# Odd mixer of a four-layer decoder on one Trainium2 core: the two softmax maps combined in one operation, the head norm taken per group inside the attention loop, its weight applied where the rows are transposed

## The reference, cut to what matters

```python
def diff_attention(q, k, v, lam):              # q, k: (B, S, H=8, 2, 64); v: (B, S, 8, 128)
    def block(qi):                             # 128 queries at a time
        s = jnp.einsum('bqhcd,bkhcd->bhcqk', qi, k).astype(jnp.float32) * scale
        p = jax.nn.softmax(s, axis=-1)
        a = p[:, :, 0] - lam * p[:, :, 1]
        return jnp.einsum('bhqk,bkhe->bqhe', a.astype(v.dtype), v)
    ...
def rms_norm(x, g):
    y = xf * lax.rsqrt(jnp.mean(jnp.square(xf), axis=-1, keepdims=True) + LN_EPS)
    return y.astype(x.dtype) * g

def odd_mixer(x, w_in, lam_p, subln_g, w_out, lam_init):
    q, k, v = jnp.split(x @ w_in, 3, axis=-1)
    q, k = rope(q), rope(k)                    # shortened
    lam = jnp.exp(jnp.sum(lp[0] * lp[1])) - jnp.exp(jnp.sum(lp[2] * lp[3])) + lam_init
    o = diff_attention(q, k, v, lam)
    o = rms_norm(o, subln_g) * (1.0 - lam_init)
    return o.reshape(B_, S, C_WIDTH) @ w_out
```

## Time and profile before

| what | value |
|---|---|
| executions timed | 3221.38, 3225.34, 3228.93 us; median 3225.34 us |
| the profiled execution's own time | 3220.99 us |
| its span in the trace, first to last instruction | 3219.2 us |
| mean granted clock of TensorE | 0.971 of full speed |
| PE busy | 3025.5 us (94%) |
| PEld, weight loads | 2511.7 us (78%) |
| POOL busy | 1751.4 us (54%) |
| DVE busy | 921.4 us (29%) |
| ACT busy | 645.0 us (20%) |
| the page's chain of work that ended last, PE's and DVE's share | 79% and 14% |

### The profile page before, as it was taken

The page is one execution under the profiler, slowest core; times in us unless marked ns, Lnnn a source line. Parts: engine busy times, 40 slices in busy tenths (PEclk is TensorE's granted clock), DMA queues, the critical chain, the costliest instruction groups (busy, mean ns, idle before and its releaser), DMA issues.

```text
span 3219.2 us, 35940 instructions
## 1 busy us (share of the span) xinstructions
PE 3025.5 (94%) x15048; PEld 2511.7 (78%) x15048; DVE 921.4 (29%) x1470; ACT 645.0 (20%) x1330; POOL 1751.4 (54%) x1472
## 2 busy tenths in 40 slices
PE   7889999999999897999999999899999998999998
PEld 6776778888887666788888887878888886788887
DVE  3535402311023295023100221833110056530102
ACT  1224212211010162122100121452010032420100
POOL 5540383566665503836666656423666665556664
PEclk9999999999999998999999999989999999899999
DMA  4221241322223202412322232002323222033232
GB/s 143 71 74 40 70 143 50 105 92 98 99 87 104 66 1 66 144 53 92 105 92 94 90 112 92 1 1 81 103 92 104 93 98 79 14 100 97 92 105 79
DMA packets 182498, 267.15 MB, mean 83 GB/s; under 512 B 6592, under 2 KB 145984, under 8 KB 182336
## 3 DMA queue, kind: packets, MB, share of 16 engines
q1 hardware_dynamic: 174240, 243.28, 22.9%
q10 hardware_dynamic: 8096, 21.56, 2.0%
HBM read 262.73 MB, written 2.10 MB: 82 GB/s over the span
## 4 chain that ended last, share of the span: by engine, by line
PE 79%; DVE 14%; POOL 3%; issue 1%; ACT 1%; DMA 1%; ACTq 0%; DVEq 0%; POOLq 0%
PE PS L464 23%; PE PS L465 23%; PE PS L466 23%; PE PS L785 3%; POOL wlo L2084 2%; DVE PS L665 2%; DVE x_row L660 1%; PE PS L771 1%; DVE nmx L1434 1%; PE PS L1324 1%; DVE xT_lo L566 1%; DVE x_row L672 1%; PE PS L917 1%; POOL whi L2079 1%; PE PS L549 1%
## 5 line engine op out<-in xcount | busy, mean ns | idle before, releaser
L2079 POOL TENSOR_SCALAR whi<-raw 128x1024 fp32r<-128x1024 f32 x460 | 485.7, 1076 | 1336.2 <-DMA raw<-ffn_w 270.0
L2084 POOL TENSOR_TENSOR wlo<-raw,whi 128x512 fp32r<-128x512 f32 x920 | 1188.5, 1328 | 0.0
L464 PE MATMUL PS<-xT_hi,whi 128*128 128x512 f32 (+1 forms) x2304 | 856.0, 372 | 41.4 <-DVE xT_lo L566 29.1
L465 PE MATMUL PS<-xT_lo,whi 128*128 128x512 f32 (+1 forms) x2304 | 848.7, 368 | 0.0
L466 PE MATMUL PS<-xT_hi,wlo 128*128 128x512 f32 (+1 forms) x2304 | 848.5, 368 | 0.0
L464 PEld LDWEIGHTS PS<-xT_hi,whi 128*128 128x128 f32 x2304 | 441.6, 192 | 118.1 <-DVE xT_lo L566 32.4
L465 PEld LDWEIGHTS PS<-xT_lo,whi 128*128 128x128 f32 x2304 | 441.6, 192 | 71.5 <-issue 2.4
L466 PEld LDWEIGHTS PS<-xT_hi,wlo 128*128 128x128 f32 x2304 | 441.4, 192 | 70.1
L464 PE MATMUL PS<-whi,xT_hi 128*128 128x512 f32 x672 | 264.5, 394 | 23.6 <-ACT a_pre L1025 16.3
L960 DVE TENSOR_TENSOR htmp<-sil,PS 128x512 f32<-128x512 f32 x88 | 56.5, 683 | 804.0 <-ACT sil L945 804.0
L464 PE MATMUL PS<-whi,h_hi 128*128 128x512 f32 x704 | 274.1, 389 | 0.0
(11 more groups left out here) (360 smaller groups left out, 3218.5 us busy)
## 6 DMA issues: line engine op xcount, KB each, us to landing
raw<-ffn_w SPq DMA_DIRECT2D x66, 1024.0 KB, 5.0
raw<-ffn_w_gu SPq DMA_DIRECT2D x44, 1024.0 KB, 5.1
raw<-ffn_w_down SPq DMA_DIRECT2D x22, 1024.0 KB, 5.0
raw<-mem_wkv SPq DMA_DIRECT2D x16, 1024.0 KB, 5.4
raw<-even_w_in SPq DMA_DIRECT2D x14, 1024.0 KB, 5.2
raw<-ev_w_in SPq DMA_DIRECT2D x14, 1024.0 KB, 5.3
raw<-odd_w_in SPq DMA_DIRECT2D x12, 1024.0 KB, 5.1
raw<-od_w_in SPq DMA_DIRECT2D x10, 1024.0 KB, 5.0
```

The source lines that it names most:

```text
L464: pe.matmul(o, lhs[0], rhs[0], start=start, stop=False, skip_group_check=True)
L465: pe.matmul(o, lhs[0], rhs[1], start=False, stop=False, skip_group_check=True)
L2079: pool.tensor_scalar(whi[b][:, cs], raw[b][:, cs], 1.0, 1.0, ALU.mult, ALU.mult).then_inc(panel_hi, 1)
L2084: m = pool.tensor_tensor(wlo[b][:, cs], raw[b][:, cs], whi[b][:, cs].bitcast(F32), ALU.subtract)
```

## The change

It does these things in `stage_odd`, and nothing in the other stages:

1. `combine` works without the first map's reciprocal. With sums s0 and s1 it forms the ratio -lam*s0/s1 (two instructions on one column) and then, in one instruction over 512 columns, map 1 times the ratio plus map 0. The result is s0 times the one before. The norm per head takes the factor out again, if its small constant is multiplied by s0 squared.
2. The norm moves into the loop, one group at a time. ACT squares the group's PSUM bank into `d_sq` (new instruction, 128x512, after the copy of unit 4g+5); `store` sums the squares per head on DVE, forms the constant times s0 squared, adds the two, waits for POOL, which raises the four columns to the power -0.5, and multiplies the bank by the result on its way to `d_row`. `store` comes two steps later (`behind` is 6 instead of 4), so groups 6 and 7 both come after the last unit.
3. The weight `subln_g` becomes one column (after the transpose a head's feature lies on the partition) and is applied, with 1 - LAM_INIT, in the copies behind the transposes: ACT's copy has it as scale, DVE's subtraction becomes one with a multiplication before it.
4. The passes after the loop (1392, 1395, 1448, 1452, 1455, 1456) are gone. With them goes the load of ACT's table for the root, which is now done in the layer norm of the output projection.
5. POOL gets the loop over the eight groups between the splits of the third and the fourth panel of the output weights.

```diff
-            pool_at.append(len(panels) + 2)
+            pool_at.append(len(panels) + (3 if st[0] == "odd" else 2))
...
+                m = act.activation(dst_hi[:, k0 + b:k0 + b + 4, 128 * t:128 * t + 128],
+                                   PS[:, bank + b // 4, :].rearrange("p (k c) -> p k c", k=4), ACT.Copy, scale=gain)
...
+                    m = dve.scalar_tensor_tensor(out=lo, in0=src, scalar=gain, in1=hi.bitcast(F32),
+                                                 op0=ALU.mult, op1=ALU.subtract)
...
-        def act_units(act, A, exps):
+        def act_units(act, A, exps, more=lambda u: None):
...
                     act.activation(A.pt(u)[:, 0:w], PS[:, A.ptb(u), 0:w], ACT.Copy).then_inc(pt_sb, 1)
+                    more(u)
...
-            behind = A.lag + 1
+            behind = A.behind
...
+            A.behind = 6
...
-                act_units(act, A, exps)
+                def squares(u):
+                    g = (u - 2) // 4
+                    if u < 5 or u % 4 != 1:
+                        return
+                    act.wait_ge(pv_done, A.u0 + 4 * g + 4)
+                    if g >= 2:
+                        act.wait_ge(sq_in, g - 1)
+                    act.activation(d_sq[:, g % 2, :], PS[:, A.ob(4 * g), :], ACT.Square).then_inc(sq_done, 1)
+                act_units(act, A, exps, squares)
+                squares(A.n + 1)
                 phase_end(act, "act")
                 load_next(act)
                 for t in range(NT):
-                    if t >= 3:
-                        act.wait_ge(sq_in, t - 2)
-                    act.activation(d_p[:, t % 3, :, :].rearrange("p a b -> p (a b)"), d_row[:, t, :], ACT.Square)\
-                        .then_inc(sq_done, 1)
-                act.wait_ge(sq_in, NT)
-                act.activation(rec[:, 0:32], rec[:, 32:64], ACT.Sqrt, scale=1.0 / 128, bias=eps_col[:, 0:1]).then_inc(sd_done, 1)
-                act_rows(act, 0, KD)
+                    act_turn(act, xT_hi, 0, KD, 2 * t, t, gain)
...
                 def combine(u):
                     dve.wait_ge(exp_done, A.u0 + u + 1)
-                    r0, r1, lr1 = (scol[:, o:o + 1] for o in range(24 + 4 * (u % 2), 27 + 4 * (u % 2)))
-                    step(dve.reciprocal(scol[:, 24 + 4 * (u % 2):26 + 4 * (u % 2)], rsum[:, 2 * u:2 * u + 2]))
-                    step(dve.tensor_tensor(lr1, r1, scol[:, 21:22], ALU.mult))
+                    ratio = scol[:, 24 + u % 2:25 + u % 2]
+                    step(dve.reciprocal(ratio, rsum[:, 2 * u + 1:2 * u + 2]))
+                    step(dve.scalar_tensor_tensor(out=ratio, in0=ratio, scalar=scol[:, 21:22],
+                                                  in1=rsum[:, 2 * u:2 * u + 1], op0=ALU.mult, op1=ALU.mult))
                     if u >= 3:
                         dve.wait_ge(pt_psum, A.u0 + u - 2)
-                    p1 = d_p[:, u % 3, 1, :]
-                    step(dve.tensor_scalar(p1, p1, lr1, None, ALU.mult))
-                    dve.scalar_tensor_tensor(out=d_a[:, u % 3, :], in0=d_p[:, u % 3, 0, :], scalar=r0,
-                                             in1=p1, op0=ALU.mult, op1=ALU.subtract).then_inc(p_ready, 1)
+                    dve.scalar_tensor_tensor(out=d_a[:, u % 3, :], in0=d_p[:, u % 3, 1, :], scalar=ratio,
+                                             in1=d_p[:, u % 3, 0, :], op0=ALU.mult, op1=ALU.add).then_inc(p_ready, 1)
...
                 def store(g, bank):
-                    return dve.tensor_copy(d_row[:, g // 2, 512 * (g % 2):512 * (g % 2) + 512], PS[:, bank, :])
+                    s0, ms, rstd_ = rsum[:, 8 * g:8 * g + 8:2], *rms_cols(g)
+                    heads = lambda ap: ap.rearrange("p (h d) -> p h d", h=4)
+                    dve.wait_ge(sq_done, g + 1)
+                    dve.tensor_reduce(ms, heads(d_sq[:, g % 2, :]), AX_X, ALU.add).then_inc(sq_in, 1)
+                    step(dve.scalar_tensor_tensor(out=rstd_, in0=s0, scalar=EPS, in1=s0, op0=ALU.mult, op1=ALU.mult))
+                    dve.wait_ge(sq_in, g + 1)
+                    dve.scalar_tensor_tensor(out=ms, in0=ms, scalar=1.0 / 128, in1=rstd_, op0=ALU.mult, op1=ALU.add)\
+                        .then_inc(rms_in, 1)
+                    dve.wait_ge(rms_root, g + 1)
+                    return dve.tensor_tensor(heads(d_row[:, g // 2, 512 * (g % 2):512 * (g % 2) + 512]), heads(PS[:, bank, :]),
+                                             rstd_.unsqueeze(2).to_broadcast([P, 4, 128]), ALU.mult)
...
+            def pool(pool):
+                for g in range(8):
+                    pool.wait_ge(rms_in, g + 1)
+                    ms, rstd_ = rms_cols(g)
+                    pool.tensor_tensor(rstd_, ms, rec[:, 16:20], ALU.pow).then_inc(rms_root, 1)
...
-                for t in range(NT):
-                    pe.wait_ge(rms_done, t + 1)
-                    pe_turn(pe, d_row[:, t, :], KD, 2 * t)
+                pe_rows(pe, d_row, 0, KD)
```

More of the change, by code:

```diff
@@ L201, in build @@
         d_pt = w("d_pt", [P, 2, 512])
-        d_sq = w("d_sq", [P, 512])
+        d_sq = w("d_sq", [P, 2, 512])
         w = Area("W")
@@ L551, in pe_turn, with act_turn @@
             m.then_inc(turned, 1)
-        def act_turn(act, dst_hi, k0, blocks, bank, t):
+        def act_turn(act, dst_hi, k0, blocks, bank, t, gain=1.0):
             n_turn["act"] += 1
@@ L557, in act_turn, with dve_turn @@
                 m = act.activation(dst_hi[:, k0 + b:k0 + b + 4, 128 * t:128 * t + 128],
-                                   PS[:, bank + b // 4, :].rearrange("p (k c) -> p k c", k=4), ACT.Copy)
+                                   PS[:, bank + b // 4, :].rearrange("p (k c) -> p k c", k=4), ACT.Copy, scale=gain)
             m.then_inc(hi_ready, 1)
-        def dve_turn(dve, dst_hi, dst_lo, k0, blocks, bank, t):
+        def dve_turn(dve, dst_hi, dst_lo, k0, blocks, bank, t, gain=None):
             n_turn["dve"] += 1
@@ L565, in dve_turn @@
             for b in range(0, blocks, 4):
-                m = dve.tensor_tensor(dst_lo[:, k0 + b:k0 + b + 4, 128 * t:128 * t + 128],
-                                      PS[:, bank + b // 4, :].rearrange("p (k c) -> p k c", k=4),
-                                      dst_hi[:, k0 + b:k0 + b + 4, 128 * t:128 * t + 128].bitcast(F32), ALU.subtract)
+                lo, hi = (dst[:, k0 + b:k0 + b + 4, 128 * t:128 * t + 128] for dst in (dst_lo, dst_hi))
+                src = PS[:, bank + b // 4, :].rearrange("p (k c) -> p k c", k=4)
+                if gain is None:
+                    m = dve.tensor_tensor(lo, src, hi.bitcast(F32), ALU.subtract)
+                else:
+                    m = dve.scalar_tensor_tensor(out=lo, in0=src, scalar=gain, in1=hi.bitcast(F32),
+                                                 op0=ALU.mult, op1=ALU.subtract)
             m.then_inc(lo_ready, 1)
@@ L733, in build @@
             lag = 3
+            behind = 4
             together = 1
@@ L1337, in stage_odd @@
                       lambda u: d_a[:, u % 3, :], lambda u: d_pt[:, u % 2, :], lambda u: u % 4 == 3)
+            A.behind = 6
             chunk = lambda c: slice(128 * c, 128 * c + 128)
             xs_ready, swapped, rope_done = S_("rope_in"), S_("rope_swapped"), S_("rope_done")
-            rms_done = S_("rms_done")
-            lam_in, lam_exp, sq_in, sq_done, sd_done = (S_(n) for n in (
-                "lam_sums", "lam_exp", "rms_sums", "rms_squares", "rms_root"))
+            lam_in, lam_exp, sq_in, sq_done, rms_in, rms_root = (S_(n) for n in (
+                "lam_sums", "lam_exp", "rms_sums", "rms_squares", "rms_in", "rms_root"))
+            gain = scol[:, 22:23]
+            rms_cols = lambda g: [rec[:, o:o + 4] for o in (8 * (g % 2), 8 * (g % 2) + 4)]
             def xs_in(n):
@@ L1403, in dve @@
                 dve.wait_ge(lam_exp, 1)
-                step(dve.tensor_tensor(scol[:, 20:21], scol[:, 18:19], scol[:, 19:20], ALU.subtract))
-                step(dve.tensor_scalar(scol[:, 21:22], scol[:, 20:21], LAM_INIT, None, ALU.add))
+                step(dve.tensor_tensor(scol[:, 20:21], scol[:, 19:20], scol[:, 18:19], ALU.subtract))
+                step(dve.tensor_scalar(scol[:, 21:22], scol[:, 20:21], -LAM_INIT, None, ALU.add))
+                step(dve.tensor_scalar(gain, pcol("subln_g"), 1.0 - LAM_INIT, None, ALU.mult))
+                dve.memset(rec[:, 16:20], -0.5)
                 dve.wait_ge(*loads["rope"])
@@ L1446, in dve @@
                 for t in range(NT):
[L1447 to L1452, removed]
-                for t in range(NT):
[L1454 to L1461, removed]
+                    dve_turn(dve, xT_hi, xT_lo, 0, KD, 2 * t, t, gain)
+            def pool(pool):
[3 more added lines that the diff above has]
+                    pool.tensor_tensor(rstd_, ms, rec[:, 16:20], ALU.pow).then_inc(rms_root, 1)
             def pe(pe):
@@ L1502, in pe @@
                 phase_end(pe, "pe")
-                for t in range(NT):
-                    pe.wait_ge(rms_done, t + 1)
```

(6 more changed lines are left out.)

2 lines of the change are left out of this document (1 added, 1 removed).

## The result

| | kernel before | changed kernel |
|---|---|---|
| median of four runs, us | 3224.67 | 3207.21 (3204.02 to 3210.88) |
| ratio, 95% interval | | 0.9945 (0.9928 to 0.9963) |
| profiled execution / span, us | 3220.99 / 3219.2 | 3204.02 / 3202.2 |
| first to last maximum of the odd mixer ("loop") | 89.70 | 89.21 |
| last maximum to first product of the output projection ("end") | 32.05 | 18.73 |

The forecast sum of 17.1 us met the profiled pair (17.0), and the forecast time of 3206 us the median. Only 13.8 us of the 17.0 lie in the changed stage, all but 0.5 of them at its end.

What follows compares the result with a forecast made beforehand. DVE was taken to bound the loop, PE 0.16 us behind per unit, with most to win in the norm's passes after it. 1.0 + 2.4 + 15.2 - 1.5 = 17.1 us gave 3203.9 or 3208.2; predicted 3206, range 3197 to 3220.

Steps and rivals of the forecast that it cites:

- first five units: Start of the odd mixer's loop: scalings go, but PE at its lower clock takes over as bound; 1.0 us gained.
- units 5 to 31: Rest of the odd mixer's loop, 26 units and 6 stores: 73.8 us before, 71.4 after, 2.4 gained.
- end, clock deduction taken off: Last maximum to output projection: 32.05 us falls to 16.83, 15.2 gained, less 1.5 for PE's clock falling before the transposes.
- outside the stage: Everything but the odd mixer: what lies behind it is only shifted as a whole; forecast 0.
- per group DVE now needs 4 x 2.18 + 2.46 = 11.18: Odd mixer's loop: four units and a store on DVE, still the bound against PE's 10.16; 11.40 before.
- P: In each store: hand-over to POOL, power and way back, hidden by nothing; 0.94 us, between 0.26 and 1.45.
- The three-operand product on one column: In each unit's combination on DVE: costed as the product it replaces, 0.20 us.
- Rival 1: Stores: POOL's power is slow and DVE waits eight times; at 5 us the kernel takes some 3240; 7%.
- Rival 2: End: PE reaches the transposes at its lower clock, costing 4.6 us instead of 1.5, 3209; 18%.
- Rival 3: First store: POOL must first fetch the power's routine, stalling DVE and PE once; 4 to 6 us, about 3211; 8%.
- Rival 4: Loop gives nothing or loses a little at P = 1.45; sum 13 us, 3210; within the forecast's own 62%.
- The table load: Layer norm of the output projection: the root's 1.28 us load moves there and costs nothing; first transposes 40.92 after projection start.

Runs made afterwards that it cites:

- e2_mult: Changed kernel with GpSimd multiplying where it takes the power, same 128x4 operands, so the norm is not computed; 3202.71 us, ratio 0.9932 to the kernel before.
- e5_after_again: The changed kernel run once more without an edit; 3210.32 us, ratio 0.9951 to the kernel before.
- e1_par128: Changed kernel with `subln_g` padded back to 128 columns, so later constants lie where they lay before; 3213.22 us, ratio 0.9962 to the kernel before.

## Why the prediction was right, and where it was not

| term | forecast | profiled pair |
|---|---|---|
| first five units | +1.0 | +1.6 |
| units 5 to 31 | +2.4 | -1.1 |
| end, clock deduction taken off | +13.7 | +13.3 |
| outside the stage | 0 | +3.2 |
| sum | 17.1 | 17.0 |

The time was met partly by luck: the gain of units 5 to 31 was forecast 3.5 us too high, and 3.2 us outside the stage, which no run gives to the change, made up for it. By the stage alone the change is worth 13.8 us, and the medians of its three kernels (3207.21, 3210.32, 3213.22) are 10 to 17 us below the kernel before in the same job.

**The end: right in its chain, lucky in its last term.** The norm's passes leave the path, DVE is 2.5 us later than before, and `mem_row` is the next wait. The last DVE instruction ended at +10.18 instead of +9.72: the last product ended at +6.68 instead of +6.48, and the last store with its dearer wait took 2.76 instead of 2.54. The store of group 6 stayed covered, by 0.06 us (1207.08 against 1207.14). From there to the projection were 8.55 us against 7.11 + 1.5. The 1.5 were deducted for the clock, but the 1.44 that came are the load's, 6.69 - 5.25. The transposes were slower by 5.35 - 3.69 = 1.66, and that cost nothing here: they were done 1.28 us before the load landed.

**The step that failed: "per group DVE now needs 4 x 2.18 + 2.46 = 11.18".** It is 4 x 2.25 + 2.70. The mechanism was right (DVE bounds, nothing hides P), two sizes were off, and they turned a small gain into a small loss. The stretch from unit 5 to 31 took 75.1 us instead of 71.4 (before: 74.0):
- "The three-operand product on one column" was costed as the plain one, 0.20; its pitch is 0.25 to 0.26. With the large combination's 0.01 a unit is 0.07 longer, 1.8 us over 26 units.
- P was 0.94; it is 0.08 + 1.01 + 0.03 = 1.12 (1.15 in the first store). With the small instructions' hundredths a store is 0.24 longer, 1.4 us over six. I had interpolated between a 128x128 product and a 128x512 subtraction, as if the work went by width. At this width the operation decides: e2_mult has the same operands at 0.20.

The two make 3.2 of the 3.5 us. Two units before the first store still ran at PE's 2.54, another 0.6, and the kernel before was 0.2 slower here than the sum has it.

**Rival 1** (slow power) falls by its size: P is 1.12, far from 3.1, though the power is dear, five times a product. **Rival 2** (clock in the gap) held half: the clock was 0.72, and 0.53 in e5_after_again, but its price of 4.6 never came. The late load covered the slow transposes in all but e1_par128, where they took 6.62 and cost at most 0.5: the load landed 6.0 us after its issue, and PE turned to it after 6.5. **Rival 3** (first power slow) falls: 1.03 against a median of 1.007, so the 6 us that the Trainium skill has for the first call of a freshly loaded routine ("GPSIMD Engine Reference", "Instruction dispatch") don't show for this operation. **Rival 4** came true in the loop, while the total hid it, but not by its reason: P is 1.12, not 1.45, and half of the miss is the unit's. **The table load** cost nothing: the first transposes of the projection came 1260.13 - 1219.19 = 40.94 us behind its start, against the 40.92 forecast.

**Left open:** why the clock falls in one execution and not in the next of the same program, and why the 1 MB load at the odd mixer's barrier mostly takes 6.0 to 6.8 us, where the same load takes 5.1 to 5.4 at the even mixer's.

## To carry to other kernels

An operation handed to an idle engine is free only if the giver has something to do meanwhile: take the result one step later, and the same power that cost 7 us in this loop costs nothing in it. Two parts of a change that meet one bound are not additive (10.4 and -0.8, or 0.4 without the fall of the clock there, against 13.8 together), so cost each against what the other leaves. Where a gain is half a per cent, compare the changed stretch in the profiles, and look at the time outside it before you credit it.

## What the hardware showed that I had not expected

- GpSimd's power on 128x4 takes 1.007 us, a product on the same operands 0.20.
- VectorE's three-operand instruction takes 0.22 us on one column where its scalar is a column in memory, and 0.15 on four columns where it is a constant (lines 1437 and 1460). No run separates the two differences.
- 32 transposes took 3.69 us behind 0.64 us of idle time (28 fillers before it) and 3.68 behind 2.89, both at a granted clock of 1.00, but 5.35, 6.47 and 6.62 behind 3.70, in executions of the same work.
- The same 1 MB load landed 6.7 us after its issue in one stage and 5.4 in another of one execution, with the other queues as good as idle (4 more packets within 35 us in the first).
